# One round copy per expert in a counted loop on TensorE, one flat loop over all rounds on VectorE and ScalarE

## The reference

```python
top_logit, top_e = lax.top_k(logits, 4)          # of 32 experts
top_w = jax.nn.softmax(top_logit, axis=-1)
...
gu = xs @ w_gu[e] + b_gu[e]                      # 1024 x 2048
gate = jnp.minimum(gate, 7.0); up = jnp.clip(up, -7.0, 7.0)
act = gate * jax.nn.sigmoid(1.702 * gate) * (up + 1)
return act @ w_dn[e] + b_dn[e]                   # 1024 x 1024
...
return jax.ops.segment_sum(y_sorted, sorted_tok, num_segments=n_tok)
```

## Time and profile before

| what | value |
|---|---|
| median of three runs | 1239.52 us (1238.1 to 1242.1) |
| span of the profiled execution | 1238.4 us |
| TensorE products busy | 980.0 us, 79% |
| VectorE busy | 449.5 us, 36% |
| ScalarE busy | 351.2 us, 28% |
| read from HBM | 466.00 MB, 377 GB/s over the span |
| mean granted TensorE clock | 0.924 |

### The profile page before, as it was taken

The page is one execution under the profiler, slowest core; times in us unless marked ns, Lnnn a source line. Parts: engine busy times, 40 slices in busy tenths (PEclk is TensorE's granted clock), DMA queues, the critical chain, the costliest instruction groups (busy, mean ns, idle before and its releaser), DMA issues.

```text
span 1238.4 us, 23246 instructions
## 1 busy us (share of the span) xinstructions
PE 980.0 (79%) x9327; PEld 492.0 (40%) x9328; DVE 449.5 (36%) x1085; ACT 351.2 (28%) x735; POOL 8.4 (1%) x20
## 2 busy tenths in 40 slices
PE   6999999978787898976859967678788676657565
PEld 3788989743233233332213322223333222212122
DVE  0656555543344244442314432323343322322212
ACT  1544424422233133331213331212332212211113
POOL 0200000000000000000000000000000000000000
PEclk9999999989999899998889989989899888988778
DMA  9979587879999989999998789999969999999994
GB/s 360 373 274 348 183 321 253 332 291 425 423 425 424 422 361 426 424 423 422 424 428 352 313 338 426 423 425 423 406 266 422 424 425 424 424 423 424 423 424 197
DMA packets 60443, 468.93 MB, mean 379 GB/s; under 512 B 5148, under 2 KB 6468, under 8 KB 24484
## 3 DMA queue, kind: packets, MB, share of 16 engines
q1 hardware_dynamic: 60324, 467.06, 91.7%
HBM read 466.00 MB, written 1.05 MB: 377 GB/s over the span
## 4 chain that ended last, share of the span: by engine, by line
PE 55%; DMA 26%; issue 12%; DVE 5%; ACT 1%; SPq 1%; DVEq 0%; ACTq 0%
PE B L1205 30%; DMA W<-in_w_down_dram 26%; PE B L953 15%; PE B L1214 4%; PE B L973 2%; PE B L1157 2%; DVE EW L880 1%; DVE EW L877 1%; DVE EW L883 1%; ACT EW L573 1%; DMA raw<-in_w_ada_dram 1%; PE B L980 1%; PE B L1262 0%; PE B L1030 0%; SPq L359 0%
## 5 line engine op out<-in xcount | busy, mean ns | idle before, releaser
L1205 PE MATMUL B<-W,mT 128*32 128x256 f32 (+1 forms) x5888 | 548.5, 519 | 89.8 <-DMA W<-in_w_gate_up_dram 37.1
L1205 PEld LDWEIGHTS B<-W,mT 128*32 128x32 f32 x5888 | 194.9, 115 | 427.7 <-issue 271.6
L584 ACT ACTIVATE hT<-hT 32x256 bf16<-32x256 bf16 x368 | 152.6, 415 | 235.4 <-DVE hT L897 227.5
L877 DVE TENSOR_SCALAR EW<-B 128x256 f32<-128x256 f32 x46 | 19.5, 425 | 420.4 <-PE B L1205 420.4
L1214 PE MATMUL B<-b_gu,mT 128*32 128x512 f32 x368 | 61.8, 731 | 138.2 <-issue 138.2
L573 ACT ACTIVATE EW<-EW 128x256 f32<-128x256 f32 x46 | 19.2, 416 | 434.6 <-DVE EW L877 434.6
L953 PE MATMUL B<-hh,wh 128*128 128x256 f32 x384 | 109.9, 286 | 0.0
L953 PE MATMUL B<-hl,wh 128*128 128x256 f32 x384 | 108.6, 283 | 0.0
L953 PE MATMUL B<-hh,wl 128*128 128x256 f32 x384 | 108.6, 283 | 0.0
L667 DVE TENSOR_TENSOR wl<-raw,wh 128x2048 fp32r<-128x2048 f32 x32 | 72.8, 2313 | 72.7 <-ACT wh L466 72.7
L466 ACT ACTIVATE wh<-raw 128x2048 fp32r<-128x2048 f32 x32 | 59.6, 1907 | 111.5 <-DMA raw<-in_w_in_dram 76.8
(11 more groups left out here) (205 smaller groups left out, 711.1 us busy)
## 6 DMA issues: line engine op xcount, KB each, us to landing
W<-in_w_gate_up_dram SPq DMA_DIRECT2D x128, 2048.0 KB, 30.1
W<-in_w_down_dram SPq DMA_DIRECT2D x63, 2048.0 KB, 23.2
raw<-in_w_in_dram SPq DMA_DIRECT2D x13, 2048.0 KB, 8.4
raw<-in_w_ada_dram SPq DMA_DIRECT2D x12, 2048.0 KB, 12.2
raw<-in_w_out_dram SPq DMA_DIRECT2D x2, 2048.0 KB, 10.2
raw<-in_w_in_dram SPq DMA_DIRECT2D x2, 1024.0 KB, 11.4
W<-in_w_down_dram SPq DMA_DIRECT2D x2, 1024.0 KB, 37.8
x_sb<-in_x_dram SPq DMA_DIRECT2D x1, 1024.0 KB, 4.8
```

Source lines behind the costliest of these rows:

```text
L584: A(ys[CAP * m:CAP * m + CAP, g * QC:(g + 1) * QC], yp[CAP * g:CAP * g + CAP, m, :], ACT.Copy).then_inc(y_moved, 1)
L877: V.tensor_scalar(halves(gs), paired(GU[:, 0:QC]), LIMIT, None, ALU.min).then_inc(gmin_ready, 1)
L1205: t = M(o, src[:, k % KQ, CAP * (k // KQ):CAP * (k // KQ) + CAP], w, start=(first and k == 0), stop=(k == KT - 1))
```

## The change

- **TensorE.** `expert` holds one copy of a round, in a loop counted by `n_rounds` (overflow rounds plus one). All rounds of an expert now release, so `released` goes up six times in every round, and every round ends with the wait for `down_done` and the `nop`. `sel_ready` is counted by rounds. The x products stand ahead of expert 31. The last round is like the others.
- **VectorE and ScalarE.** One loop over all `total` rounds. VectorE loads the number of the next round's expert from `expert_of` in each round. It sets `sel` in each round, and lowers `pos` at the end of a round for the next one instead of at the start.
- **The table.** VectorE computes it on all 128 partitions, with a running sum over experts (`upto`). From this come `total`, `freed` and, with a compare against the partition number and a reduction, the owner of each round. TensorE turns the owner column into a row with one small product, for which it waits (`owner_ready`) between the weights' transposes and the turn of `hg`.
- **SyncE** waits for `released` counted from `freed[e]` = 6 x (rounds up to and with e, less one), so that again only the last round's releases let a load go. It loads that base once per expert.

The core of the diff:

```diff
-            sp.wait_ge(released, TURN * UNITS * i + u - SLOTS + 1)
+            if u == SLOTS or (u - SLOTS) % UNITS == 0:
+                before = freed_before(TURN * i + (u - SLOTS) // UNITS)
+            sp.wait_ge(released, before + ((u - SLOTS) % UNITS + 1))
...
+            one(G_.iota(pcol, pattern=[[1, 1]], base=0, channel_multiplier=1, ...), c_pcol)
...
-            act.wait_ge(table_ready, 1)
-            with nc.Fori(0, TURNS, engines=[act.engine], hint_back_edge=True) as i:
-                for r in range(TURN):
-                    expert(TURN * i + r)
-            expert(E - 2)
-            expert(E - 1, last=True)
+            act.wait_ge(table_ready, 2)
+            n_all = act.value_load(total, min_val=E, max_val=ALL_ROUNDS)
+            with nc.Fori(0, n_all, engines=[act.engine], hint_back_edge=True) as n:
+                one_round(n)
...
-            V.tensor_copy(rounds[:, :], nover).then_inc(table_ready, 1)
+            V.tensor_scalar(n_rounds, nover[0:1, :], 1.0, None, ALU.add).then_inc(table_ready, 1)
+            V.memset(unit_row, 1.0).then_inc(dve_step, 1)
+            steps[0] += 1
+            dve.wait_ge(dve_step, steps[0])
+            step(V.tensor_tensor_scan(upto, unit_row, nover, 0.0, ALU.add, ALU.add))
+            V.tensor_copy(total, upto[0:1, E - 1:E]).then_inc(table_ready, 1)
+            V.tensor_scalar(freed, upto[0:1, :], float(UNITS), -float(UNITS), ALU.mult, ALU.add).then_inc(table_ready, 1)
+            dve.wait_ge(c_pcol, 1)
+            step(V.tensor_scalar(passed, upto, pcol[:, 0:1], None, ALU.is_le))
+            step(V.tensor_reduce(owner, passed, AX.X, ALU.add))
+            V.tensor_scalar(owner, owner, float(E - 1), None, ALU.min).then_inc(owner_ready, 1)
...
+            def one_round(n):
+                e = dve.value_load(expert_of[0:1, ds(n + 1, 1)], min_val=0, max_val=E - 1)
+                dve.wait_ge(gathered, n + 1)
+                dve.wait_ge(pos_moved, n + 1)
+                select(e)
...
+                select_weighted(e)
+                select_bias(e)
+                dve.wait_ge(sw_ready, TA * n + 2 * TA)
+                V.tensor_scalar(pos[:, :, ds(e, 1)], pos[:, :, ds(e, 1)], -float(CAP), None, ALU.add).then_inc(pos_moved, 1)
...
+            pe.wait_ge(owner_ready, 1)
+            M(B[5][0:1, 0:P], owner, ident[:, :], start=True, stop=True).then_inc(owner_done, 1)
             pe.wait_ge(hg_ready, 1)
-            pe.wait_ge(table_ready, 1)
             turn(G, hg, hTg_done)
...
-                stream(Db[:, 0:QC], actT, down_rows, u0 + NQ, turns, True, done, split).then_inc(down_done, 1)
-                if done:
-                    pe.wait_ge(down_done, n + 1)
-                    pe.nop().then_inc(released, 1)
+                stream(Db[:, 0:QC], actT, down_rows, u0 + NQ, turns, True, split).then_inc(down_done, 1)
+                pe.wait_ge(down_done, n + 1)
+                pe.nop().then_inc(released, 1)
...
-                more = pe.value_load(rounds[0:1, ds(e, 1)], min_val=0, max_val=MAXR - 1)
-                with pe.If(more > 0):
-                    with pe.Fori(0, more):
-                        one_round(e, r, turns, False, last)
-                one_round(e, r, turns, True, last, last)
+            def expert(e, r, turns, split=False):
+                more = pe.value_load(n_rounds[0:1, ds(e, 1)], min_val=1, max_val=MAXR)
+                with pe.Fori(0, more):
+                    one_round(r, turns, split)
```

More of the change, by code:

```diff
@@ L156, in hybrid_trunk @@
         shl = mod[:, 0, 12 * E + 64:13 * E + 64]
-        over = mod[0:1, 0, 0:E * (MAXR - 1)].rearrange("p (e m) -> p e m", e=E)
-        nover = mod[0:1, 0, E * (MAXR - 1):E * MAXR]
+        over = mod[:, 0, 0:E * (MAXR - 1)].rearrange("p (e m) -> p e m", e=E)
+        nover = mod[:, 0, E * (MAXR - 1):E * MAXR]
+        unit_row = mod[:, 0, E * MAXR:E * MAXR + E]
+        upto = mod[:, 0, E * MAXR + E:E * MAXR + 2 * E]
+        passed = mod[:, 0, E * MAXR + 2 * E:E * MAXR + 3 * E]
+        owner = mod[:, 0, E * MAXR + 3 * E:E * MAXR + 3 * E + 1]
+        rounds = mod[0:1, 1, 0:5 * E + 1].bitcast(i32)
+        pcol = stat[:, 50:51]
+        n_rounds = rounds[:, 0:E]
+        freed = rounds[:, E:2 * E]
+        total = rounds[:, 2 * E:2 * E + 1]
+        expert_of = rounds[:, 3 * E:3 * E + ALL_ROUNDS + 1]
         UNITS = 6
@@ L416, in _ @@
                         allow_small_or_imprecise_dtypes=True), c_iota)
+            one(G_.iota(pcol, pattern=[[1, 1]], base=0, channel_multiplier=1,
+                        allow_small_or_imprecise_dtypes=True), c_pcol)
             pool.wait_ge(s_ws, 16)
@@ L860, in _ @@
+            V.tensor_scalar(pos[:, :, 0:1], pos[:, :, 0:1], -float(CAP), None, ALU.add).then_inc(pos_moved, 1)
             dve.wait_ge(hTg_done, 1)
             V.tensor_copy(hTg, G[:, 0:QC].rearrange("p (q s) -> p q s", q=KQ)).then_inc(hTg_ready, 1)
[L862 to L875, removed]
+            dve.wait_ge(owner_done, 1)
@@ L905, in one_round @@
                     V.tensor_tensor(ys[2 * CAP:3 * CAP, g * QC:(g + 1) * QC], yr[rows_, :], yp[rows_, 1, :], ALU.subtract).then_inc(y_low, 1)
[L906 to L919, removed]
+            dve.wait_ge(table_ready, 2)
+            n_all = dve.value_load(total, min_val=E, max_val=ALL_ROUNDS)
+            with nc.Fori(0, n_all, engines=[dve.engine], hint_back_edge=True) as n:
+                one_round(n)
             dve.wait_ge(s_gfin, 16)
@@ L1186, in _, with stream @@
             pe.reg_mov(rnd, 0)
-            def stream(dst, src, rows_of, u0, turns, first, done, split=False):
+            def stream(dst, src, rows_of, u0, turns, first, split=False):
                 per = KQ if rows_of is gate_up_rows else 2 * KQ
@@ L1206, in stream @@
                               start=(first and k == 0), stop=(k == KT - 1))
-                    if done and k % per == per - 1 and k < KT - 1:
+                    if k % per == per - 1 and k < KT - 1:
                         t.then_inc(released, 1)
@@ L1230, in wait_outputs, with one_round @@
                 pe.wait_ge(st_ready, n + 1)
-            def one_round(e, r, turns, done, split=False, last=False):
+            def one_round(r, turns, split):
                 n = pe.snap(rnd, min_val=0, max_val=ALL_ROUNDS)
                 u0 = UNITS * r
-                pe.wait_ge(sel_ready, e + 1)
+                pe.wait_ge(sel_ready, n + 1)
                 pe.wait_ge(hTg_ready, n + 1)
                 bias()
[L1240 to L1244, removed]
-                wait_outputs(n)
-                t = scatter()
-                if done:
[L1248 to L1253, removed]
+                stream(GU, hTg, gate_up_rows, u0, turns, False).then_inc(gu_done, 1)
+                pe.wait_ge(yw_ready, n + 1)
+                pe.wait_ge(s_ready, TA * n + 2 * TA)
+                gather()
+                wait_outputs(n)
+                scatter().then_inc(released, 1)
                 pe.wait_ge(act_ready, n + 1)
                 turn(Xb, ua, actT_done)
-                if not last:
-                    pe.wait_ge(hg_ready, n + 2)
-                    turn(G, hg, hTg_done)
+                pe.wait_ge(hg_ready, n + 2)
+                turn(G, hg, hTg_done)
                 pe.wait_ge(sw_ready, TA * n + TA)
@@ L1281, in _ @@
             expert(E - 2, 0, TURNS)
-            expert(E - 1, 1, TURNS, last=True)
+            for a in range(TA):
+                for h in range(NH):
+                    M(Yb[a][h][:, :], ident[:, :], x_sb[:, a, h * HALF:(h + 1) * HALF],
+                      start=False, stop=True, skip_group_check=True)
+            expert(E - 1, 1, TURNS, split=True)
             n = pe.snap(rnd, min_val=0, max_val=ALL_ROUNDS)
             pe.wait_ge(swT_ready, n + 1)
+            pe.wait_ge(hTg_ready, n + 1)
             keep_warm(WARM_CUT, G)
```

52 lines of the change are left out of this document (21 added, 31 removed).

## The result

The changed kernel takes 1220.6 us (median of four runs, 1220.39 to 1220.69) against 1239.3 us before: a ratio of 0.984, 95% interval 0.983 to 0.985. I had forecast 1240.2 with a range that ended at 1229.5. The profiled execution has a span of 1218.6 us and took 1220.39.

What follows compares the result with a forecast made beforehand. Time was taken as weight bytes at 425 GB/s plus five DMA gaps (43 us), a start and a tail. Terms -5.6 + 7.9 - 1.6 = +0.7 us gave 1240.2 us, range 1229.5 to 1246.

Steps and rivals of the forecast that it cites:

- Part 1: TensorE's jumps over the second copy go; only expert 0's, at the start of the expert stage, counts: -5.6 us.
- gap A: Idle of the DMA engines at 265 to 280 us, 7.2 us; expert 0's jump is on its path.
- Part 2: TensorE now waits for its products in every round: 0.88 us a round, nine times on the path, +7.9 us.
- D: DMA idle at 700 to 720 us, 14.2 us, set by TensorE's rounds; two drains inside expert 14, idle near 15.9.
- B and C: DMA idle at 450 to 465 us (4.3 us) and 665 to 675 us (4.8 us); two drains each, idle near 6.2.
- Part 3: TensorE's outer back edge, 2.5 to 3.4 us, stays as slow with five copies as with ten: 0 us.
- the rival that the shorter loop stays in the instruction memory: TensorE's five copies are kept: 8.6 us off at expert 20, code transfers another 1.9, 1229.7 us; chance 0.22.
- F: DMA idle at 895 to 915 us, 12.6 us, set by TensorE's rounds; outer back edge and three drains on its path.
- Part 4: Halved TensorE code transfers, some 0.7 MB at 425 GB/s in the saturated stretches: -1.6 us, bounds 0 and -3.5.
- Part 5: One flat loop each on VectorE and ScalarE gains nothing; the extra work lies in time spent waiting.
- Part 6: SyncE reads a base once per expert between issues, before an already long wait: nothing.
- rivals b to d: ScalarE stalls leaving its loop, 1244.5 us, 0.13; first-pass code stall, 1243.6, 0.09; drain hidden, 1232.3, 0.06.

Runs made afterwards that it cites:

- experiment 7: Wait for down_done and a nop added to overflow rounds of the kernel before: 1250.1 us; then that wait and nop taken out of the changed kernel: 1208.6 us.
- pad 30: Changed kernel with 15 dummy transposes (30 instructions), always jumped over, ahead of each expert's counted loop on TensorE: 1239.6 us.
- pad 90: Changed kernel with 45 dummy transposes (90 instructions), always jumped over, ahead of each expert's counted loop on TensorE: 1237.2 us.
- experiments 2 and 4: Changed kernel with ten experts per turn instead of five: 1234.1 us; changed kernel with jumped-over dummy transposes per expert, 30 or 90 instructions: 1239.6 and 1237.2 us.

## Why the prediction was wrong

- **Part 1, jumps and the start: right.** -5.6 us forecast, gap A -5.3, and +6.1 with the jump put back. The jumps under saturated weights left no other mark than their code.
- **Part 2, the drain: right in mechanism and price.** 0.88 us a round in the kernel before, nine on the path, +7.9 in the gaps. In the changed kernel D grew by 2.3 (forecast 1.8). B and C were to grow by 1.8 each and changed by +0.2 and -1.0. In experiment 7, with late landings as before, they did grow by 1.7 and 1.6; so I read the difference as landings that are now 1.8 us less late, which is argued. What I missed is the drain's share at the boundaries: all of 1.58 us and not 0.73. That doesn't move this change's sum, but it is why taking the drain out gave 12 us.
- **Part 3, the outer back edge: this step failed.** I took 0 and gave 0.22 to the rival that the shorter loop stays in the instruction memory. It does, up to about 1,773 instructions and not at about 1,873. The loop has 1,718, so it fits by a margin of under 10%. The forecast describes a kernel whose loop doesn't fit: with pad 30 and pad 90 the same change measured 1239.6 and 1237.2 us, against 1240.2 forecast. The rival's terms for F held: forecast -8.6, and F went from 12.3 to 5.7 with three drains of +2.6 in it, so -9.2. My argument against it (the code is read only shortly ahead) said how far the sequencer reads ahead, not how long it keeps what it has read. By the rule of the Trainium skill ("Runtime: NRT & Kernel Launch", Instruction fetch mechanics: 2048 instructions in blocks of 256, as a FIFO) five copies were a border case, and they fell on the near side; the runs put the edge between 1,773 and 1,873, below that figure.
- **Part 4, the code traffic: mis-sized, in the forecast and in the rival.** I priced it by bytes (0.7 MB at 425 GB/s: -1.6 us, at most -3.5). The packets that went hold 1.39 MB, 3.3 us by that price, but outside the gaps the weight stream gained 9.0 us, plus what B and C did not grow by. A code packet of 16 KB holds its engine 1.08 us, while the weights move at 26.6 GB/s on an engine (0.62 us for as much), and a unit lands with its slowest part. This is why even the rival's 1229.7 us was 9 us too high, and the measured time outside my range: it had -3.5 us for code where 9.0 came outside the gaps, and +3.6 us for B and C where -0.8 came. That code traffic slows the weights is shown (1254.7 against 1220.6 us, and the 62, 71 and 77 packets of experiments 2 and 4 with rates between); that it explains all 9.0 us is argued from rates and landings.
- **Part 5, flat loops: right**, nothing either way. ScalarE now loads its activation table in each round (46 instead of 8 times, 1.28 us each), in time that it spends waiting.
- **Part 6, SyncE: right, and rivals b to d rightly held small.** ScalarE's table load follows its last copy without a pause, there was no stall in the first pass, and the drain isn't hidden.

## What to carry to other kernels

When the weights bound a kernel, look at the few places where their stream runs dry, and ask of each edit on another engine whether it ends one of them earlier. Count the instructions of an outer loop: here it either stayed in the instruction memory or was read anew in each turn, and unexecuted code counted like any other. A wait for an engine's own products costs more than the idle that it shows (0.80 us), since the sequencer can't do its next work under them: here 0.88 us in front of a plain back edge and 1.58 in front of a load of the count. Letting the consumer wait for the semaphore instead took both away.

## What the runs showed of the hardware

- TensorE's loop of up to about 1,773 instructions is kept (back edge 0.23 us, 24 packets in the whole program); with about 1,873 each turn is read anew (71 packets), and the first jump behind the back edge takes 4.7 to 5.0 us.
- A taken jump over 340 instructions that haven't been read costs 6.06 us while weights stream. The clock then falls, and the bias products take 1.94 us instead of 1.06.
- Code traffic of an engine that nobody waits for (60 packets of 8 KB in some 300 us) made the kernel 34 us longer, by a lag of the weights' landings that grew by about 0.5 us a packet. The same instructions in a loop cost nothing (1220.6 us).
- A code packet of 16 KB took 1.08 us, a weight packet of that size 0.62.
